# A two-block transformer kernel on one core: x turned once in advance, twelve column tiles beside the first modulation chunks, TensorE's modulation loads moved to the stream queue

## The chip, the cores and the metric

The kernel runs on one core of one Trainium2 chip. The metric is the device time of one execution in microseconds (us). Before the change three runs gave 2236.53, 2239.11 and 2246.66, so the median is 2239.11 us.

## The reference, cut to what matters

The reference runs two blocks on x (256 tokens by 2048 features, float32). The first block has two layers, the second one has one. Only the first block is touched by the change:

```python
for l in range(2):
    mod = silu(c) @ w_ada[l] + b_ada[l]                  # 2048 x 6144 weights
    shift, scale, gate = split(mod, 3)
    h = layernorm(x) * (1 + scale) + shift
    p = h @ w_in[l]                                      # columns: u_f 1024, z_f 1024, cq 512, ckv 256, k_r 64, z_a 1024
    y_f = real(fft2(u_f by groups of 128)) @ w_fmix[l] * silu(z_f)
    q = rmsnorm(cq) @ w_q_b[l];  kv = rmsnorm(ckv) @ w_kv_b[l]
    y_a = attention(q, kv, rope(k_r)) * silu(z_a)        # 8 heads
    x = layernorm(alpha * x + gate * (concat(y_f, y_a) @ w_out[l])) * ln_g[l] + ln_b[l]
```

The modulation is a product of one vector with a matrix: it uses each of its weights once. The other products work on all 256 tokens.

## The kernel before, in words

**Stream.** All large weights but the modulation's lie in one stream of 1 MB chunks (128 partitions by 2048 floats), in the order in which TensorE uses them; layer 0 uses chunks 0 to 56 (`PER_LAYER`, line 57), layer 1 the next 57. SP's queue loads them into a ring of three (`raw`, `RAW`, line 48; `load`, line 328): the load of chunk g waits until chunk g-3 is split. ScalarE casts a chunk to `w_hi` (line 964), VectorE subtracts that to make `w_lo` (line 1378), into one of two slots; a slot is free when TensorE has used the chunk two before (`weights_used`). Each product is three matmuls, lo by hi, hi by lo, hi by hi (`mm3`, lines 409 to 411).

**Modulation.** Layer 0's shift and scale weights are 32 chunks of their own (`ada0`), loaded by SP into a ring of three (lines 320 to 348), with 8 stream chunks between them. TensorE multiplies each chunk in `ada_chunk` (line 586) into one bank. Four chunks make one row of 512 results; ScalarE copies the finished row (`take_row`, line 1006) before TensorE may begin the next, and TensorE turns it into columns (`turn_row`, line 598). VectorE adds the bias (`read_mod0`). The other 64 chunks (layer 0's gate and layer 1's shift and scale, 48 chunks, then layer 1's gate, 16) are loaded by POOL's queue (`weights`, line 369) into a ring of two slots. In layer 0 the even ones go to VectorE (`add_ada`, line 1405; the first of a sum is line 1402), the odd ones to TensorE (`ada_add`, line 539). POOL's loop waits for VectorE's add and loads the next even chunk, then waits for TensorE's add and loads the next odd one, in turn.

**Start of layer 0.** SP loads three modulation chunks, then x. VectorE takes the statistics (line 1496), and stages the normalized x by quarters of 512 features (`stage`, line 1451); TensorE turns a quarter of it after each eighth modulation chunk (`turn_tokens`, line 459). ScalarE applies scale and shift from PSUM (`modulated`, line 989), and VectorE splits the result into `a_hi` and `a_lo` (`split_modulated`, line 1460). From modulation chunk 12 on TensorE does one piece behind each chunk. A piece (`piece`) is one contraction tile of 128 by four column tiles, twelve matmuls of 256 columns. There are eight early column tiles: q's latents (4), kv's latents (2), the rope key, and the first u tile. They take 32 pieces, k outer: 20 beside the modulation chunks, 12 behind.

**Fourier groups.** Then come w_fmix with the channel DFT (chunk 8, four products of 512 columns), the first z tile, and eight groups: a u chunk, the sequence DFT of the group before (`seq_dft`), a z chunk, and the turn to tokens (`to_tokens`). A chunk of this kind is 48 matmuls of 256 columns. ScalarE takes u, the tanh of z, t and y in hi parts, VectorE the lo parts, gates and products, each in an order written out by hand.

**Heads.** For each of eight heads TensorE does `project` (its chunk), the first half of the gate chunk, the turn of the last head's softmax (`turn`, line 746), the second half, the scores, and `attend` of the last head, and in layer 0 then an `ada_add`. VectorE's `head` does the q and k parts, its own `add_ada`, half a split, the turned softmax, the other half, then, when `attend` is done, y (line 1633), the gate (line 1644), v, and the split of the next chunk but one.

**Output projection.** Sixteen chunks of 24 matmuls of 512 columns (`token_chunk`). In layer 0 there are 8 adds of each engine beside them (`W_ADDS`), the sums by rows (`finish_rows`, `turn_rows`, `spread_rows`) and the read of the gate (`read_gate`). VectorE adds the residual by blocks (`z_block`).

## Time and profile before

| what | value |
|---|---|
| median of three runs | 2239.11 us |
| the profiled execution's own time | 2246.86 us |
| its span in the profile | 2245.1 us |
| TensorE busy (matmul) | 2083.1 us, 93% |
| VectorE busy | 1380.8 us, 62% |
| ScalarE busy | 914.7 us, 41% |
| moved by DMA | 462.18 MB, mean 206 GB/s |
| chain that ended last | TensorE 83%, VectorE 9%, DMA 4%, ScalarE 2% |

The span is what the profiler saw of the program on the core; 1.8 us of the execution lie around it. Busy times of different engines overlap, so they do not add up to the span. The chain is followed back from the last instruction, at each step to what released it. Matmuls are pipelined: one of 256 columns shows a duration of 287 ns, though the next starts earlier. The stages of the part that the change touches are: modulation stage of layer 0, 0 to 135.7 us; early tiles and Fourier groups to 305.9; heads to 408.9; output projection to 543.7; layer 1 from there.

### The profile page before, as it was taken

To read this page: it belongs to the slowest core of one execution; us is meant where nothing else is said; L and a number is where in the kernel's file an instruction comes from. 1 tells how busy PE (TensorE), PEld (TensorE's weight loads), DVE (VectorE), ACT (ScalarE), POOL (GpSimd) and SP (SyncE) were. 2 spreads that over 40 slices of the span, in tenths; PEclk is the share of its full clock that TensorE was granted. 3 is DMA by queue.
4 is the path that set the end of the run, shared out by engine and by line. 5 is a ranking of instruction groups with operands and counts; after the bars stand their busy time and mean duration, and the time that the engine had idled before them with its cause. 6 is when DMAs were issued, how large, how long until landed. Compare 5 with 4: busy or idle time off the path is not lost.

```text
span 2245.1 us, 37841 instructions
## 1 busy us (share of the span) xinstructions
PE 2083.1 (93%) x14348; PEld 1885.5 (84%) x14348; DVE 1380.8 (62%) x1895; ACT 914.7 (41%) x1350; POOL 39.0 (2%) x77
## 2 busy tenths in 40 slices
PE   4889899886989999799999899989999999999998
PEld 1578789664989997599998899879989989988986
DVE  4236667557579675779998555555545545555555
ACT  2234345422444564343434333445434434443443
POOL 0000000000000000000000000000000000000000
PEclk7799999988999999889999999999999999999999
DMA  8867767574567544434544455554555555555553
GB/s 360 322 263 300 282 245 290 197 299 187 198 259 284 208 159 169 150 128 173 183 172 150 156 183 185 188 190 147 187 189 186 187 192 188 183 199 191 183 192 131
DMA packets 64198, 462.18 MB, mean 206 GB/s; under 512 B 7120, under 2 KB 7632, under 8 KB 8176
## 3 DMA queue, kind: packets, MB, share of 16 engines
q1 hardware_dynamic: 53696, 385.33, 46.9%
q0 software_dynamic: 10416, 75.63, 8.9%
q8 instruction: 64, 1.05, 0.2%
q14 instruction: 22, 0.18, 0.0%
HBM read 458.83 MB, written 2.10 MB: 205 GB/s over the span
## 4 chain that ended last, share of the span: by engine, by line
PE 83%; DVE 9%; DMA 4%; ACT 2%; issue 2%; DVEq 0%; ACTq 0%; POOLq 0%; SPq 0%; POOL 0%
PE ps L409 26%; PE ps L410 26%; PE ps L411 26%; DMA area<-in_ada 4%; DVE w_lo L1378 3%; PE ps L586 2%; ACT w_hi L964 1%; PE ps L539 1%; PE ps L459 1%; DVE area L1405 1%; DVE X L1758 0%; PE ps L598 0%; DVE X L1752 0%; PE ps L746 0%; DVE ln L1799 0%
## 5 line engine op out<-in xcount | busy, mean ns | idle before, releaser
L1378 DVE TENSOR_TENSOR w_lo<-raw,w_hi 128x1024 fp32r<-128x1024 f32 x658 | 777.5, 1221 | 470.7 <-ACT w_hi L964 469.1
L964 ACT CAST w_hi<-raw 128x1024 fp32r (+1 forms) x658 | 656.8, 1047 | 568.1 <-PE ps L411 567.7
L409 PE MATMUL ps<-a_hi,w_lo 128*128 128x256 f32 (+1 forms) x2912 | 835.9, 287 | 14.3 <-DVE y_lo L1386 5.8
L410 PE MATMUL ps<-a_lo,w_hi 128*128 128x256 f32 (+1 forms) x2912 | 830.8, 285 | 0.0
L411 PE MATMUL ps<-a_hi,w_hi 128*128 128x256 f32 (+1 forms) x2912 | 829.5, 285 | 0.0
L409 PEld LDWEIGHTS ps<-a_hi,w_lo 128*128 128x128 f32 x2912 | 559.7, 192 | 37.6 <-issue 22.2
L411 PEld LDWEIGHTS ps<-a_hi,w_hi 128*128 128x128 f32 x2912 | 559.3, 192 | 0.0
L410 PEld LDWEIGHTS ps<-a_lo,w_hi 128*128 128x128 f32 x2912 | 556.9, 191 | 0.7 <-issue 0.5
L409 PE MATMUL ps<-w_hi,y_lo 128*128 128x512 f32 x768 | 304.7, 397 | 2.6 <-DVE st L1386 2.6
L410 PE MATMUL ps<-w_lo,y_hi 128*128 128x512 f32 x768 | 302.4, 394 | 0.0
L411 PE MATMUL ps<-w_hi,y_hi 128*128 128x512 f32 x768 | 301.8, 393 | 0.0
L409 PEld LDWEIGHTS ps<-w_hi,y_lo 128*128 128x128 f32 x768 | 146.1, 190 | 43.8 <-issue 7.9
L411 PEld LDWEIGHTS ps<-w_hi,y_hi 128*128 128x128 f32 x768 | 146.3, 191 | 31.3
L410 PEld LDWEIGHTS ps<-w_lo,y_hi 128*128 128x128 f32 x768 | 146.3, 191 | 29.7 <-issue 0.2
L1405 DVE SCALAR_TENSOR_TENSOR area<-area,csil 128x2048 f32<-128x2048 f32 x36 | 84.5, 2346 | 29.2 <-DMA area<-in_ada 29.1
L1317 ACT ACTIVATE sc<-ps 128x256 f32<-128x256 f32 x64 | 24.6, 385 | 178.4 <-PE ps L411 178.4
L2015 DVE TENSOR_TENSOR sc<-sc 128x256 f32<-128x256 f32 x64 | 27.3, 426 | 103.0 <-ACT sc L1317 103.0
L409 PE MATMUL ps<-y_hi,w_lo 128*128 128x256 f32 x272 | 78.3, 288 | 9.8 <-DVE y_lo L1931 7.3
L586 PE MATMUL ps<-area,csil 128*1 128x512 f32 x256 | 44.6, 781 | 36.3 <-DMA area<-in_ada 25.1
L410 PE MATMUL ps<-y_lo,w_hi 128*128 128x256 f32 x272 | 77.9, 286 | 0.0
L411 PE MATMUL ps<-y_hi,w_hi 128*128 128x256 f32 x272 | 77.9, 286 | 0.0
L1386 DVE TENSOR_TENSOR st<-ps,st 128x256 fp32r<-128x256 f32 (+1 forms) x98 | 48.0, 505 | 32.4 <-ACT st L1083 22.0
(235 smaller groups left out, 1953.8 us busy)
## 6 DMA issues: line engine op xcount, KB each, us to landing
raw<-in_stream SPq DMA_DIRECT2D x331, 1024.0 KB, 4.8
area<-in_ada POOLq DMA_DIRECT2D x64, 1024.0 KB, 5.4
area<-in_ada SPq DMA_DIRECT2D x32, 1024.0 KB, 7.2
grow<-in_rows POOLq DMA_DIRECT2D x4, 1024.0 KB, 5.0
area<-in_rows POOLq DMA_DIRECT2D x4, 1024.0 KB, 7.0
X<-in_x SPq DMA_DIRECT2D x1, 2048.0 KB, 13.5
out<-X SPq DMA_DIRECT2D x4, 512.0 KB, 2.7
con<-in_consts SPq DMA_DIRECT2D x1, 129.5 KB, 13.1
```

What stands on the lines that cost most here:

```text
L409: pe.matmul(o, w[1], a[0], start=first, stop=False, skip_group_check=shared)
L410: pe.matmul(o, w[0], a[1], start=False, stop=False, skip_group_check=shared)
L411: return pe.matmul(o, w[0], a[0], start=False, stop=last, skip_group_check=shared)
L459: o = pe.transpose(bank(turn_banks(n, q)[i // 2], i % 2 * T + t * P, P), src, ident)
L539: o = pe.matmul(ps[32 * j:32 * j + 1, ROW_BANK[r] * 512:(ROW_BANK[r] + 1) * 512], csil[:, KT + n % KT:KT + n % KT + 1], ada_ring[:, CH + j ...
L586: o = pe.matmul(ps[32 * k:32 * k + 1, 2 * 512:3 * 512], csil[:, at:at + 1], ada0_slot(c % 3)[:, k * 512:(k + 1) * 512], start=s == 0, stop ...
L964: ac.copy(to, raw[:, bass.ds((g % RAW) * CH + h * n, n)]).then_inc(hi_ready, 1)
L1317: ac.activation(sc[:, b * T:(b + 1) * T], bank(b), ACT.Relu).then_inc(f_relu, 1)
L1378: ve.tensor_tensor(to, raw[:, bass.ds((g % RAW) * CH + h * n, n)], hi.bitcast(F32), ALU.subtract).then_inc(lo_ready, 1)
L1386: return ve.tensor_tensor(out_, exact, hi.bitcast(F32), ALU.subtract)
L1405: ve.scalar_tensor_tensor(out=ada_acc, in0=chunk, scalar=c, in1=ada_acc, op0=ALU.mult, op1=ALU.add).then_inc(ada_step, 1)
L2015: ve.tensor_tensor(s, r, r, ALU.mult).then_inc(f_sq, 1)
```

## The change

In words, part by part:

- **Order of the first loads.** SP loads x and the constants before the first three modulation chunks.
- **x turned in advance.** VectorE stages all four quarters at once; TensorE turns them after modulation chunks 2 to 5; ScalarE copies the turned quarter to a hi part (in `y_hi`, not yet used), VectorE subtracts to make the lo part (in `y_lo`). `modulated` then reads the hi part, and VectorE adds the lo part times scale, one operation for each tile.
- **Twelve early column tiles.** u tiles 1 and 2, z tiles 0 and 1, kv's latents, the rope key, u tile 0, and q's latents, three chunks to a quarter. That makes 48 pieces. Behind modulation chunk c, pieces up to (c - 10) * 3 // 2 are done, so 31 by chunk 31. SP loads 9 stream chunks in this stage. The last quarter is mixed with the w_fmix products (`last_quarter`). u tiles 1 and 2 are kept in hi and lo, z tile 1's gate is kept in `grow`. Layer 1 gets the same tiles and order.
- **Groups.** Group loops are written out in full on all engines; groups begin with z tile 2, then u tile 3.
- **TensorE's modulation chunks.** POOL's loop loads only the even chunks for layer 0's time. SP loads the odd ones (`row_weights`) between stream chunks, into the same slot of the ring. TensorE's adds stand behind the chunks in `PE_ADDS` (6 in the groups, 10 in the heads, 8 in the output projection), in the heads ahead of `attend`.
- **VectorE's adds.** In layer 0: 5 in the groups, 7 in the heads, 12 in the output projection (before: 9, 7 and 8). In layer 1: two in each of groups 4 to 7 and one in each head (before: two in each of the eight groups).
- **Banks and order of the row sums** follow from that.

The diff, cut to its core:

```diff
-FIRST = 8
-L_FMIX = FIRST
-L_DFT = FIRST + 2
-L_FOUR = FIRST + 1
+FIRST = 3
+L_FMIX = 4 * FIRST - 1
+L_Z2 = L_FMIX + 2
+L_DFT = L_Z2 + 1
+L_FOUR = L_DFT + 1 - 6
 L_HEAD = L_FOUR + 2 * GROUPS
...
-W_ADDS = ((1, 3, 4, 6, 8, 10, 12), (3, 4, 5, 6, 7, 8, 10, 12))
+PE_ADDS = tuple(L_FOUR + i for i in (7, 8, 10, 11, 12, 14)) \
+    + tuple(L_HEAD + i for i in (1, 3, 5, 7, 8, 9, 11, 12, 13, 15)) \
+    + tuple(L_OUT + i for i in (2, 4, 5, 7, 8, 10, 11, 12))
...
             sp.dma_start(vec[:, :], vectors).then_inc(vec_in, 16)
+            sp.dma_start(X[:, :].rearrange("p (t d) -> p t d", t=2), x.rearrange("(t p) d -> p t d", p=P))\
+                .then_inc(x_in, 16)
+            sp.dma_start(con[:, :], consts).then_inc(con_in, 16)
             for c in range(3):
                 sp.dma_start(ada0_slot(c), ada0[c]).then_inc(ada0_landed[c], 16)
...
+            early = {9: 0, 11: 1, 14: 2, 17: 3, 19: 4, 22: 5, 25: 6, 27: 7, 30: 8}
             for c in range(3, ADA0):
+                if c in early:
+                    g = early[c]
+                    load(g, g % 2, g >= 2)
                 sp.wait_ge(ada0_used, c - 2)
                 sp.dma_start(ada0_slot(c % 3), ada0[c]).then_inc(ada0_landed[c % 3], 16)
...
+            def row_weights(i):
+
+                sp.dma_start(ada_ring[:, CH:2 * CH], ada[2 * i + 1]).then_inc(ada_rowed, 16)
+
+            for g in range(9, PER_LAYER + 1):
+                load(g, g % 2, True)
+                if g == L_FMIX + 1:
+                    sp.wait_ge(ada0_used, ADA0)
+                    row_weights(0)
+                if g - 5 in PE_ADDS[:-1]:
+                    i = PE_ADDS.index(g - 5) + 1
+                    sp.wait_ge(ada_pe, i)
+                    row_weights(i)
...
             weights(0, 0)
-            weights(1, 1)
-            pool.wait_ge(ln_lo, 8)
+            pool.wait_ge(y_mul, 2)
             row(grow[:, :], R_GATE, grow_in)
             with pool.Fori(1, 3 * KT // 2) as i:
-                for par in range(2):
-                    pool.wait_ge((ada_step, ada_pe)[par], i)
-                    weights(2 * i + par, par)
+                pool.wait_ge(ada_step, i)
+                weights(2 * i, 0)
...
+                if 2 <= c < 6:
+                    turn_tokens(0, c - 2)
...
-                if c % 8 == 7:
-                    turn_tokens(0, c // 8)
-                if c >= 12:
-                    n = c - 12
-                    if n == 0:
-                        pe.wait_ge(ln_var, NORM["meta"] + 1)
-                    piece(0, n // 8, n % 8 // 4, n % 4)
...
+                if c == 10:
+                    pe.wait_ge(ln_var, NORM["meta"] + 1)
+                    pe.wait_ge(xn_l, 4)
+                while p < (c - 10) * 3 // 2:
+                    piece(0, p // 12, p % 12 // 4, p % 4)
+                    p += 1
+            while p < 36:
+                piece(0, p // 12, p % 12 // 4, p % 4)
+                p += 1
+                if p == 34:
+                    turn_row(ADA0 // 4 - 1)
+            last_quarter(0)
...
+            def last_quarter(l):
+
+                pieces(l, 3, 0)
+                pieces(l, 3, 1, range(2))
+                if l:
+                    pe.wait_ge(fm_y, 2 * KT)
+                else:
+                    pe.wait_ge(col_in, 4)
+                half(l * PER_LAYER + L_FMIX, 1)
+                fourier_weights(l, (0, 1))
+                pieces(l, 3, 1, range(2, 4))
+                fourier_weights(l, (2, 3))
+                pieces(l, 3, 2)
...
+                def later(o):
+
+                    if l == 0 and o in PE_ADDS:
+                        ada_add(2 * PE_ADDS.index(o) + 1)
+
+                def group_u(q):
+                    g = L_FOUR + 2 * q
+                    chunk(G + g, slot_of(g), bank(0), a_ops)
+                    later(g)
...
+                to_tokens(0)
+                group_z(2)
+                seq_dft(0)
+                to_tokens(1)
...
+                for q in range(4, GROUPS):
+                    group_u(q)
+                    seq_dft(q - 1)
+                    group_z(q)
                     to_tokens(q)
...
                     project(h, first)
+                    if l == 0:
+                        later(L_HEAD + 2 * h)
...
-                    if l == 0 and h == HEADS - 1:
-                        finish_rows(3)
+                    if l == 0:
+                        later(L_HEAD + 2 * h + 1)
+                        if h == 3:
+                            finish_rows(2)
                     if not first:
                         attend(h - 1, second)
...
+                    later(L_OUT + c)
+                    if l == 0 and c == 4:
+                        finish_rows(3)
+                    if l == 0 and c == 6:
+                        turn_rows(4, 10)
...
+            for q in range(3):
+                split(3 * q, q % 2, q % 2)
                 ac.wait_ge(col_in, q + 1)
                 modulated(0, q)
+                take_row(2 * q + 2)
+                split(3 * q + 1, (q + 1) % 2, (q + 1) % 2)
+                split(3 * q + 2, q % 2, q % 2)
+                take_row(2 * q + 3)
...
+                if n == 0:
+                    for m in (2 * i, 2 * i + 1):
+                        one = pair[:, m % 2 * T:(m % 2 + 1) * T]
+                        o = ve.scalar_tensor_tensor(out=one, in0=y_lo[:, m * T:(m + 1) * T].bitcast(F32),
+                                                    scalar=mod[:, KT + m:KT + m + 1], in1=one, op0=ALU.mult, op1=ALU.add)
+                    own.link(o)
...
+                    if l:
+                        add_ada(7 * KT // 2 + h, h % 2, 2 * KT + h)
+                    elif h < 3:
+                        add_ada(10 + 2 * h, 0, 5 + h)
+                    elif h > 3:
+                        add_ada(8 + 2 * h, 0, 4 + h, 3 if h == 4 else 0)
...
-                    if l == 0 and c in W_ADDS[0]:
-                        n = 2 * KT + 2 + 2 * W_ADDS[0].index(c)
-                        add_ada(n, 0, n // 2)
+                    if l == 0 and (c < 4 or 5 <= c < 13):
+                        n = 24 + 2 * c - 2 * (c > 4)
+                        add_ada(n, 0, n // 2, 4 if c == 5 else 0)
```

## Rows read from the trace of the kernel before

**Rows 1.** The page: its span, and TensorE's and the others' busy time.
```profile
span 2245.1 us, 37841 instructions
PE 2083.1 (93%) x14348; PEld 1885.5 (84%) x14348; DVE 1380.8 (62%) x1895; ACT 914.7 (41%) x1350; POOL 39.0 (2%) x77
```
**Rows 2.** Stages: window, length, busy PE, PEld, DVE, ACT, POOL; clock, DMA share, GB/s.
```profile
0.00:52.91 52.91, 22.65 (x123) 5.44 (x124) 22.83 (x54) 12.75 (x19) 0.20 (x4) 0.72 0.88 355
52.91:71.40 18.49, 15.87 (x96) 10.04 (x96) 1.45 (x2) 2.48 (x3) 0.00 (x0) 0.78 1.01 424
71.40:88.40 17.00, 14.38 (x88) 9.17 (x88) 4.74 (x9) 4.41 (x7) 0.00 (x0) 0.80 0.67 256
...
124.51:135.68 11.17, 11.17 (x77) 7.23 (x78) 0.91 (x1) 0.00 (x0) 0.00 (x0) 0.85 0.84 344
...
305.86:408.86 103.00, 101.69 (x850) 93.65 (x849) 78.22 (x120) 57.53 (x119) 6.89 (x13) 1.00 0.79 295
408.86:543.73 134.87, 119.01 (x538) 87.47 (x538) 77.80 (x80) 39.18 (x49) 8.47 (x16) 0.91 0.66 250
```
**Rows 3.** Timeline of TensorE in the modulation stage: start, length, instruction, idle before.
```profile
52.91 1.88 PE L586 MATMUL ps<-area,csil 128*1 128x512 f32 x8 [2.42 <-DMA area<-in_ada]
...
71.40 1.88 PE L586 MATMUL ps<-area,csil 128*1 128x512 f32 x8 [2.62 <-ACT rs L1006]
73.21 1.87 PE L598 MATMUL ps<-csil,rs 128*128 128x1 f32 x8
...
80.59 1.04 PE L586 MATMUL ps<-area,csil 128*1 128x512 f32 x8
```
**Rows 4.** Timeline of VectorE, 0 to 56 us: statistics of x, rotary table.
```profile
16.23 4.84 DVE L1496 BATCH_NORM_STATS2 ln<-X 128x6 f32<-128x512 f32 x8 [12.24 <-DMA X<-in_x]
...
39.06 0.35 DVE L1535 TENSOR_SCALAR rope<-rope,con 128x256 f32<-128x256 f32 x1 [3.93 <-ACT rope L1016]
```
**Rows 5.** Timeline of TensorE in one head: add, gate chunk, turn, scores, add.
```profile
348.92 1.04 PE L539 MATMUL ps<-area,csil 128*1 128x512 f32 x8
...
354.88 0.33 PE L409 MATMUL ps<-a_hi,w_lo 128*128 128x256 f32 x1
...
357.79 0.60 PE L746 MATMUL ps<-con,sc 128*128 128x128 f32 x4
...
361.03 0.28 PE L409 MATMUL ps<-st 128*128 128x256 f32 x1
...
363.27 1.04 PE L539 MATMUL ps<-area,csil 128*1 128x512 f32 x8
```
**Rows 6.** Timeline of VectorE in the same head: add, y, split.
```profile
357.98 2.35 DVE L1405 SCALAR_TENSOR_TENSOR area<-area,csil 128x2048 f32<-128x2048 f32 x1
...
363.47 0.42 DVE L1633 SCALAR_TENSOR_TENSOR sc<-ps,zs 128x256 f32<-128x256 f32 x1 [0.27 <-PE ps L411]
...
365.01 2.36 DVE L1378 TENSOR_TENSOR w_lo<-raw,w_hi 128x1024 fp32r<-128x1024 f32 x2 [0.33 <-ACT w_hi L964]
```
**Rows 7.** Landings: two POOL loads (180 us), one SP load (141), POOL in output projection.
```profile
DMA to landing us min/median/max: 5.1/6.1/7.0
...
DMA to landing us min/median/max: 4.9/4.9/4.9
...
DMA to landing us min/median/max: 5.0/6.8/9.2
```
**Rows 8.** Timeline of TensorE: two modulation adds behind a wait.
```profile
272.34 1.89 PE L539 MATMUL ps<-area,csil 128*1 128x512 f32 x8 [9.01 <-DMA area<-in_ada]
...
471.44 1.88 PE L539 MATMUL ps<-area,csil 128*1 128x512 f32 x8 [3.78 <-DMA area<-in_ada]
```
**Rows 9.** The view of rows 2, the 4 us behind the second of these waits.
```profile
472.00:476.00 4.00, 4.00 (x15) 2.17 (x8) 2.39 (x2) 0.00 (x0) 0.53 (x1) 0.50 0.87 279
```
**Rows 10.** Timeline of VectorE: its first modulation add in the output projection.
```profile
424.71 1.28 DVE L1402 TENSOR_SCALAR area<-area,csil 128x2048 f32<-128x2048 f32 x1
```
**Rows 11.** TensorE's waits in layer 1, 568.64 to 760 us: total, times, longest.
```profile
PE ps L409 <- DVE st L1386: 4.8, 3, 2.2
```

More of the change, by code:

```diff
@@ L1726, in head @@
                     ve.reciprocal(stat[:, 6:8], stat[:, 4:6]).then_inc(s_sum, 1)
-                head(0, True, l == 0)
-                with own.loop(1, HEADS - 1, 1) as h:
-                    head(h, False, l == 0)
-                head(HEADS - 1, False, False)
+                for h in range(HEADS):
+                    head(h, h == 0)
                 def z_block(j, t):
```

571 lines of the change are left out of this document (318 added, 253 removed).

## The prediction, made before the changed kernel was seen

> **What bounds the kernel now.** I read the page first [rows 1]: TensorE is busy 93% of the span, so nearly everything that takes work off its path, or stops it, moves the end. Then the engines' time by stage [rows 2]. In the first 135.7 us 32 chunks of layer 0's shift and scale weights stream in, and TensorE is paced by others. In the heads of layer 0 (305.86 to 408.86) it is busy 101.69 of 103.00, in the output projection behind them (408.86 to 543.73) only 119.01 of 134.87. What to see in [rows 3]: in the first stage each row of four modulation chunks costs TensorE a wait of 2.62 for ScalarE's copy of the row, and then some microseconds at half clock (a chunk's matmuls take 1.88 instead of 1.04).
>
> **Part 1: x turned in advance, twelve tiles.**
> (a) SP's queue now loads x before the modulation chunks. VectorE got x at 16.23 [rows 4], behind 3 MB of chunks; a megabyte more of queue lands 2.5 later (below, [rows 7]), so x comes 7.5 earlier, at 8.7. From x to the finished rotary table took 39.06 - 16.23 = 22.8; four stagings and four subtractions are put in between, 4 x (1.0 + 1.2) as estimates from the 0.42 and 0.6 us operations of [rows 6] and [rows 4] by their sizes. The table is ready near 41, the first modulated pair near 47.6. Chunk 12, at 52.91 before [rows 3], starts near 50: **-2.9**.
> (b) From chunk 12 on, rows of four chunks carry six pieces instead of four. A 256-column matmul costs TensorE (361.03 - 354.88 - 0.45 for the turn at 357.79) / 48 = 0.1187 [rows 5], a piece of twelve 1.42. A row at full clock: four chunks 4.0, the turned row 1.0 (1.87 at half clock, [rows 3]), six pieces 8.6, together 13.6. ScalarE now copies the row before its cast and not behind it, and TensorE has a piece to do meanwhile, so the waits of 2.62 go. Five rows took 135.7 - 52.9 = 82.8 (a plain one 17.00, [rows 2]); they would take 68 at full clock and 85 at this row's mean clock of 0.80. I take 75, since the long waits came just before the half clock: **-7.8**. In this stage SP loads 9 stream chunks instead of 8.
> (c) 31 pieces are done by the last modulation chunk instead of 20. The products in all are the same, so afterwards 11 x 12 x 0.1187 = **-15.7**. The last quarter keeps its waits (for the last modulation and for the Fourier weights, now behind a Tanh table load) and gets one more, on the split of its third chunk: **+1.0**. VectorE's two corrections for each of eight pairs (0.42 each) lie in its idle time; without that cover they cost 7.
> Part 1 together: -25.4. Bounds: -32 (full clock) to -15 (clock of before).
>
> **Part 2: the odd modulation chunks on the stream queue.** That queue is in order. Let a be the stream chunk after which TensorE did the add before. The next odd chunk is issued behind stream load a+5, which waits until chunk a+2 is split, and that split begins only when a is consumed. A lone 1 MB load by SP lands in 4.9; of two issued 0.6 apart, the second landed 7.0 + 0.6 - 5.1 = 2.5 after the first [rows 7]. So the odd chunk lands 7.3 to 7.4 after the split of a+2. Two chunks later that is in time; at the very next chunk it is not. Neighbours in the new list, by offset in the layer: 16-17, 19-20, 20-21 (groups), 32-33, 33-34, 36-37, 37-38 (heads), 45-46, 48-49, 51-52, 52-53 (output projection).
> Heads. Project runs from 348.92 + 1.0 to 354.88, 5.0; the gate chunk to 361.03; scores 1.42, attend 0.71, add 1.0 [rows 5]. The add now stands ahead of attend. VectorE's chain y, gate, v, split begins when attend ends (363.2) and ends at 365.01 + 2.36, 4.1 later [rows 6]. For 32-33: scores 1.4, add 1.0, row sum 1.0, attend 0.7 and 4.1 make 8.2; the load goes at 8.4 and lands at 15.7. TensorE is there after 4.1 + 5.0 = 9.1 and waits 6.6; for 36-37, one row sum less on both sides, the same. For 33-34 the split of 35 is cut in two by the softmax turn, which now stands behind the stalled add: 7.6 + half a chunk 2.85 + turn 0.45 + copy and subtraction 1.4 + half a split 1.2 = 13.5, landed 21.0. TensorE is there at 7.6 + 2.85 + 0.45 + 2.85 + 1.42 = 15.2 and waits 5.8; 37-38 the same. Together 24.8. Nothing is gained in exchange, the loads were in time here. After a wait of 3.78 an add took 1.88 [rows 8], and the clock stood at 0.50 for the next 4 us [rows 9]; I count 2.6 lost after each wait, 10 for four. Heads: **+35**. From below, with the split 4.1 after the chunk and no clock lost, 9; from above 45.
> Groups. Gone is the wait of 9.01 [rows 8] with some 3 of half clock. New, by the same sum with the add not ahead of attend: 3.8 at 16-17, 5.5 at 19-20, and 5 of clock: **+2** (-8 to +8).
> Output projection. VectorE makes 12 adds here instead of 8, all through one ring slot, each 2.35 [rows 6]; the next load is issued 0.6 behind it. TensorE, with 5.7 for a chunk and 1.0 for an add, is slower than this cycle only if a load lands within 3.7. POOL's loads here took 5.0 at least and 6.8 in the median [rows 7], many issued two at once; alone I take 5.8, a cycle of 8.7. The first add ends 18.2 into the stage (424.71 + 2.35, [rows 10]); eleven more take 95; the two last chunks and a row sum 12: 125. The neighbours' waits lie partly beside this; I count 10 of them: 135, against 134.87. **0** (-15 to +26).
>
> **Part 3: layer 1.** Its 16 adds stood two to a group; eight now go to the heads, where layer 0 bore one each. TensorE waited 4.8 there on VectorE's subtractions [rows 11], and lost some clock: **-4** (0 to -8).
>
> Sum: -25.4 + 2 + 35 + 0 - 4 = +8 on the profiled execution's 2246.9 (span 2245.1). That execution lies 7.8 above the median of the runs, so the same 8 goes on 2239.1: **2247**.
>
> **Rivals.** A measurement of this kernel can tell about 0.5%, 11 us, from no change.
> A, the forecast: what the first stage gains is given back in the heads. 2247, its own range 2229 to 2262. Chance 0.38.
> B, slower: the output projection becomes VectorE's chain of modulation loads. Place: its adds from chunk 1 to chunk 12. If SP's two loads for each chunk delay POOL's, a landing takes 8.2, between the median and the longest 9.2 [rows 7], and not 5.8; 11 x 2.4 = 26 makes 2273. It decides from a landing of 6.1 on. For it speaks that median, against it that many of these loads went in pairs. 0.32. The Trainium skill (DMA: Bandwidth & Descriptors, Queues, rings and completion order) says that each DMA engine goes round the queues that have work, packet by packet. By that rule POOL's load would share its way with SP's two, and B would hold.
> C, faster: the odd chunks land in time in the heads. Then the heads cost -1 and the total is 2211. For it: SP's new wait blocks nothing; against it: the sum above. 0.22.
> D, the change does not do what it says: the first stage's loads bind, and the products are not free. At 355 GB/s (0 to 52.91, [rows 2]) its 45.5 MB last 128 and start 3 late; chunk 31 ends 7 later than I take, the total is 2254. Against it: 424 GB/s from 52.91 to 71.40 [rows 2]. 0.08. The skill's rule (same page, Where 436 GB/s comes from) that reads from HBM bind a core at about 358 GB/s is this case. The 424 of this trace disagrees with it.
>
> **How the numbers follow.** A: same 0.34, faster and slower 0.02 each; B: slower 0.30, same 0.02; C: faster 0.20, same 0.02; D: slower 0.06, same 0.02. Faster 0.22, same 0.40, slower 0.38. The range reaches down to C and up to near B: 2211 to 2270.
>
> **What would show it.** TensorE waits 6 us before its modulation matmuls at four places in the heads, ended by SP's load, and the heads take near 138 instead of 103; in the first stage no wait of 2.62, rows near 15, the last chunk done near 125; in the output projection VectorE waits for its load at nearly every add. If TensorE waits nowhere in layer 0's heads, A falls and C holds; if the output projection takes over 145, B; if the first stage ends later than 132, D.

## The result, and the profile after

The changed kernel took 2256.68 us in the median of six runs (2253.37 to 2257.75), the kernel before 2239.21 in the median of six (2236.53 to 2246.66). The ratio is 1.0072, 95% interval 1.0056 to 1.0088: slower by 0.78%, 17.5 us. The forecast was 2247, the range 2211 to 2270. The profiled execution of the changed kernel took 2257.66, 1.0 above its median, that of before 7.7 above its own, so the two spans differ by 10.8 only; the last experiment deals with the other 6.7.

The page of the changed kernel, its span and busy times; it answers to [rows 1].

```profile
span 2255.9 us, 37129 instructions
PE 2078.6 (92%) x14348; PEld 1879.9 (83%) x14348; DVE 1391.3 (62%) x1913; ACT 921.5 (41%) x1355; POOL 26.2 (1%) x53
```

TensorE's busy time fell by 4.5 us (2083.1 before) and its idle time rose by 15.3 (from 162.0 to 177.3). The granted clock averages 0.956 over the span, before it was 0.955: the half clock that left the first stage came back in later ones.

The stages of the changed kernel, with the columns of [rows 2]: to modulation chunk 12, the 20 chunks behind it, early tiles and groups to the first head's add, heads, output projection.

```profile
0.00:51.22 51.22, 28.76 (x159) 10.39 (x159) 29.42 (x64) 16.86 (x23) 0.20 (x4) 0.81 0.97 390
51.22:120.70 69.48, 69.34 (x550) 48.88 (x549) 25.82 (x36) 20.26 (x26) 0.00 (x0) 0.99 0.97 399
120.70:274.11 153.41, 134.77 (x1066) 124.63 (x1062) 93.26 (x126) 64.16 (x101) 4.36 (x8) 0.94 0.61 228
274.11:412.39 138.28, 113.39 (x874) 99.15 (x873) 76.19 (x117) 57.85 (x119) 3.17 (x6) 0.89 0.60 227
412.39:558.51 146.12, 121.89 (x546) 88.46 (x546) 86.90 (x83) 39.07 (x49) 6.87 (x13) 0.88 0.73 273
```

The same five stages of the kernel before, in its profiled execution. Two of the rows stand in [rows 2]; here are the other two that the accounting needs:

```profile
52.91:135.68 82.77, 72.29 (x445) 46.26 (x446) 15.12 (x22) 13.76 (x20) 0.00 (x0) 0.78 0.81 324
135.68:305.86 170.18, 154.97 (x1236) 141.69 (x1235) 105.55 (x131) 68.68 (x107) 11.79 (x22) 0.96 0.70 260
```

So the change gained 31.8 us up to the first head's add (305.86 to 274.11), paid 35.3 in the heads (103.00 to 138.28) and 11.3 in the output projection (134.87 to 146.12), and gained 4.0 behind it (1701.4 to 1697.4, each span less the end of the projection): +10.8 in all.

The modulation stage, TensorE's timeline of the changed kernel; it answers to [rows 3].

```profile
65.81 1.04 PE L655 MATMUL ps<-area,csil 128*1 128x512 f32 x8
66.78 1.05 PE L667 MATMUL ps<-csil,rs 128*128 128x1 f32 x8
```

No wait of 2.62 stands before the first chunk of a row, and chunk and turn take 1.04 and 1.05, not 1.88 and 1.87: the clock is whole (0.99 in the window above, 0.78 before).

TensorE's waits of the changed kernel in the heads, then in the output projection (what waited, for what: total, times, longest):

```profile
PE ps L608 <- DMA area<-in_ada: 23.6, 4, 6.3
...
PE ps L608 <- DMA area<-in_ada: 15.2, 4, 7.7
PE ps L452 <- DVEq L1555: 5.4, 1, 5.4
PE ps L617 <- DVE area L1536: 3.5, 1, 3.5
```

Two of those adds in TensorE's timeline, one of the groups and one of the heads; they answer to [rows 8]:

```profile
226.03 1.89 PE L608 MATMUL ps<-area,csil 128*1 128x512 f32 x8 [10.03 <-DMA area<-in_ada]
```
```profile
330.46 1.88 PE L608 MATMUL ps<-area,csil 128*1 128x512 f32 x8 [6.33 <-DMA area<-in_ada]
```

Each took 1.88 or 1.89, not 1.04: it ran at half clock, as after the waits of before. L608 is TensorE's modulation add, L452 a matmul on stream weights, L617 the row sum, L1536 VectorE's modulation add, L1555 its read of the gate. In the heads only a wait of 1.3 us stands beside these, as before (103.00 less 101.69 busy). So 23.6 of the 35.3 that the heads lost are waits, and 11.7 are busy time (113.39 against 101.69). Part of that is half clock, and part is more work: TensorE's adds in the heads, before and then in the changed kernel (eight records are one add; behind the count stand busy us, the mean ns of one, and the idle time before):

```profile
L539 PE MATMUL ps<-area,csil 128*1 128x512 f32 x56 | 7.3, 591 | 0.0
L608 PE MATMUL ps<-area,csil 128*1 128x512 f32 x80 | 13.8, 769 | 23.6 <-DMA area<-in_ada 23.6
```

These are 7 adds and 10, so three more, some 2.9 us at full clock; they came out of the groups, which had 9 and have 6. That leaves some 8.8 for the half clock. SP's seven loads for adds in the heads, the four that were waited for among them:

```profile
DMA to landing us min/median/max: 6.8/6.8/6.9
```

Each of the four was issued 0.4 us behind a stream load (the two at 323.1 and 323.5, for instance, landed 4.6 and 6.9 after their issue).

### The profile page after: what moved, and what is told of

It is laid out like the page before. It is cut to its first block, busy times and chain, and to the rows that moved or that the text cites. A ratio compares the mean times of both kernels' runs of the same rounds, so it can differ in the third digit from the quotient of the medians.

```text
span 2255.9 us, 37129 instructions
## 1 busy us (share of the span) xinstructions
PE 2078.6 (92%) x14348; PEld 1879.9 (83%) x14348; DVE 1391.3 (62%) x1913; ACT 921.5 (41%) x1355; POOL 26.2 (1%) x53
## 4 chain that ended last, share of the span: by engine, by line
PE 77%; DVE 12%; DMA 7%; ACT 2%; issue 1%; SPq 0%; ACTq 0%; DVEq 0%; POOLq 0%
PE ps L452 25%; PE ps L453 24%; PE ps L454 24%; DMA area<-in_ada 6%; DVE w_lo L1509 4%; DVE area L1536 2%; PE ps L655 1%; PE ps L608 1%; ACT w_hi L1038 1%; DVE st L1517 1%; DVE X L1940 0%; PE ps L502 0%; DMA raw<-in_stream 0%; DVE X L1934 0%; ACT sc L1269 0%
## 5 line engine op out<-in xcount | busy, mean ns | idle before, releaser
L452 PE MATMUL ps<-a_hi,w_lo 128*128 128x256 f32 (+1 forms) x2912 | 830.4, 285 | 10.6 <-DVE w_lo L1509 6.7
L452 PEld LDWEIGHTS ps<-a_hi,w_lo 128*128 128x128 f32 x2912 | 555.1, 191 | 32.2 <-issue 21.9
L452 PE MATMUL ps<-w_hi,y_lo 128*128 128x512 f32 x768 | 306.0, 398 | 8.0 <-DVEq L1555 5.4
L452 PEld LDWEIGHTS ps<-w_hi,y_lo 128*128 128x128 f32 x768 | 146.9, 191 | 49.4 <-issue 9.7
L1536 DVE SCALAR_TENSOR_TENSOR area<-area,csil 128x2048 f32<-128x2048 f32 x36 | 84.5, 2346 | 32.2 <-DMA area<-in_ada 32.2
L452 PE MATMUL ps<-y_hi,w_lo 128*128 128x256 f32 x272 | 78.7, 289 | 8.8 <-DVE y_lo L2111 5.8
L608 PE MATMUL ps<-area,csil 128*1 128x512 f32 x192 | 31.7, 739 | 53.5 <-DMA area<-in_ada 53.4
```

What stands on the lines that cost most here:

```text
L452: pe.matmul(o, w[1], a[0], start=first, stop=False, skip_group_check=shared)
L608: o = pe.matmul(ps[32 * j:32 * j + 1, ROW_BANK[r] * 512:(ROW_BANK[r] + 1) * 512], csil[:, KT + n % KT:KT + n % KT + 1], ada_ring[:, CH + j ...
L1536: ve.scalar_tensor_tensor(out=ada_acc, in0=chunk, scalar=c, in1=ada_acc, op0=ALU.mult, op1=ALU.add).then_inc(ada_step, 1)
```

## The experiments

Times of one run each are compared with the changed kernel's profiled 2257.7; where there is a median, it is of four runs. The six runs of the changed kernel spread over 4.4 us, so a single run that differs by 6 or 7 says little by itself; there the stage that was aimed at carries the argument.

**1. The row load one stream load earlier.**

```diff
-                if g - 5 in PE_ADDS[:-1]:
-                    i = PE_ADDS.index(g - 5) + 1
+                if g - 4 in PE_ADDS[:-1]:
+                    i = PE_ADDS.index(g - 4) + 1
```

> TensorE's modulation weights are asked for one stream load earlier, ahead of the stream load they follow now. In the changed kernel the loads for two adds in neighbouring places are issued 0.4 us behind a stream load and land 6.8 to 6.9 us later, and TensorE waits 6.33, 5.56, 6.19 and 5.50 us for them in heads and 10.03 us at chunks 19 to 20 of the groups, with the granted clock at half after each. Theory: the place of the issue is all that is wrong. Issued at the end of the add before, alone, the load lands in 4.9 us while TensorE does its next chunk (some 6.4 us): the four waits (23.6 us) and the half clock behind them (some 10 us) go, and heads take 103 to 106 us instead of 138.3; of the groups' 14.7 us of waits more than half goes; in all 2200 to 2220 us, below the kernel before. Rival 1: the adds themselves, ahead of the attend step and of the scores, are what costs: heads stay above 125 us and the time moves by less than 10 us. Rival 2: SyncE now waits for an add and holds the stream loads behind it, so TensorE waits for its stream chunks instead: the idle places move, heads 120 us or more and the time 2235 or more.

Measured: 2208.25 us in the median (2204.88 to 2208.83), beside 2238.65 for the kernel before; ratio 0.9853, 0.9826 to 0.9880. The stages from the first kernel's same marks, groups, heads and output projection:

```profile
120.50:261.14 140.64, 132.02 (x1066) 123.64 (x1063) 93.06 (x126) 63.85 (x101) 4.35 (x8) 0.99 0.67 250
261.14:371.87 110.73, 106.34 (x874) 95.70 (x873) 76.15 (x118) 57.74 (x119) 3.17 (x6) 0.98 0.75 282
371.87:507.96 136.09, 117.55 (x546) 85.81 (x546) 86.63 (x83) 39.18 (x49) 6.85 (x13) 0.92 0.79 295
```

TensorE's waits in its heads, and the landing of SP's loads there:

```profile
PE ps L608 <- DMA area<-in_ada: 3.1, 1, 3.1
...
DMA to landing us min/median/max: 4.7/6.4/7.8
```

Two characters of the source are worth 48 us. The theory holds in its main point, and both rivals fall: with the same adds in the same places, asking earlier for their loads turned four waits of 23.6 us in the heads into one of 3.1, and no wait for a stream chunk came in exchange. The stream loads did get slower: those of the heads landed in 6.0 us in the median instead of 4.8. Of the gain, 27.6 lies in the heads (138.3 to 110.7), 12.8 in the groups, 10.0 in the output projection. One detail of the theory was off: the loads do not land in 4.9, but in 6.4 in the median. They are in time because they start sooner, not because they are much faster (6.8 in the changed kernel). Heads stayed 7.7 above before and not 0 to 3: 3.1 is the one wait, some 1.7 the half clock behind it (3.4 us long), and some 2.9 the three more adds that stand there (874 records against 850, eight to an add).

**2. The add behind attend.**

```diff
+                    if not first:
+                        attend(h - 1, second)
                     if l == 0:
                         later(L_HEAD + 2 * h + 1)
                         if h == 3:
                             finish_rows(2)
-                    if not first:
-                        attend(h - 1, second)
```

> In heads, TensorE's second modulation add (and the finishing of one row) stands behind the attend step of the head before instead of ahead of it; loads as in the changed kernel. If the four head waits are set by the landing of the load (asked for 0.4 us behind a stream load, 6.8 us to land), the add comes some 1 us later in its head and the load for the next one too: the waits stay between 4 and 6 us each, heads take 132 to 140 us (138.3 now), the time falls by 8 us at most. If it is the place ahead of attend that costs, since VectorE and ScalarE idle while TensorE waits there, heads fall to 125 us or less and the time by over 12 us.

Measured: 2249.96, 7.7 less, with heads of 135.0 (273.95 to 408.93). TensorE's waits in its heads:

```profile
PE ps L608 <- DMA area<-in_ada: 19.4, 4, 5.4
```

4.5 to 5.4 each. The place ahead of attend cost a microsecond a time (23.6 less 19.4, by four), and the rest of each wait is the lateness of the load. The theory's numbers for the waits, the stage and the time are all met, the time as far as one run tells.

**3. Short loads for VectorE in the output projection.**

```diff
-            with pool.Fori(1, 3 * KT // 2) as i:
+            with pool.Fori(1, 13) as i:
                 pool.wait_ge(ada_step, i)
                 weights(2 * i, 0)
+            with pool.Fori(13, 3 * KT // 2) as i:
+                pool.wait_ge(ada_step, i)
+                pool.dma_start(ada_ring[:, 0:CH // 4],
+                               ada[bass.ds(2 * i, 1), :, 0:CH // 4].rearrange("a p n -> (a p) n")).then_inc(ada_landed[0], 16)
```

> GpSimd's loads of modulation weights from the fourteenth on (those that VectorE adds in the output projection, and one before) move a quarter of each chunk only; the rest of the buffer keeps older weights, so the sums of these chunks are not computed in full. VectorE's adds are as long as before, and everything else is the changed kernel's. Theory (the chain of load and add on VectorE made the output projection 146.1 us instead of 134.9): the landings fall from 6.3 us on average to some 3 us, VectorE's waits for them (26 us there) go nearly all, TensorE's waits of 3.47 to 7.71 us at 452 to 519 us shrink under 2 us each, and the output projection takes 128 to 136 us: the time falls by 10 to 18 us. Rival: the adds and the gate read themselves (2.3 us each, queued ahead of a split) hold TensorE up: the output projection stays above 142 us.

The kernel leaves out three quarters of the weights of those chunks, so it is a probe and not a version. Measured: 2250.99, 6.7 less and not 10 to 18; the heads, which the edit does not aim at, were 2.0 longer in this execution. Its output projection:

```profile
415.28:550.73 135.45, 116.59 (x546) 84.66 (x546) 86.53 (x83) 39.08 (x49) 6.97 (x13) 0.94 0.62 229
```

VectorE's waits for these loads in the output projection, in the changed kernel, then here; and GpSimd's landings, the same two:

```profile
DVE area L1536 <- DMA area<-in_ada: 26.6, 8, 6.1
```
```profile
DVE area L1540 <- DMA area<-in_ada: 10.7, 5, 4.7
```
```profile
DMA to landing us min/median/max: 5.0/5.4/9.3
```
```profile
DMA to landing us min/median/max: 3.2/4.1/5.3
```

The stage fell by 10.7, to within a microsecond of before, inside the theory's 128 to 136 and far from the rival's 142: VectorE's adds took as long as before, so it is the loads in the chain load, add, load on VectorE that made it long. The landings came down to 4.1 only, not to 3; VectorE still waited 10.7 us of 26.6; and TensorE's waits for its own row loads stayed at 4.2 to 5.0 (three), not under 2. With the time these are four numbers of the theory that were too good. The first experiment reached 136.1 by the other end, with full loads on VectorE and TensorE's loads early. The stage is long where both chains are late at once; mending either one brings it to about 136.

**4. Five early pieces for four chunks instead of six.**

```diff
-                while p < (c - 10) * 3 // 2:
+                while p < (c - 10) * 5 // 4:
```

> In the modulation stage five pieces of the first mixer's chunks are laid beside every four modulation chunks from the tenth on, instead of six: 26 pieces by the last chunk instead of 31, so that five (each 12 products, 1.42 us at full clock) run behind it. If TensorE's work alone sets the stage, nothing is lost: the last modulation chunk ends some 7 us earlier (120.7 now, 114 then) and the first head's add stands at 274 us as now. If the weight loads (1 MB each) set it, the last chunk ends at 118 or later and the five pieces are added behind: the first head's add at 277 to 281 us, the time 3 to 7 us longer.

Measured: 2279.04, 21.4 more, and the first head's add at 292.65: far outside both. TensorE's waits in the stage, and ScalarE's timeline at the same time:

```profile
86.32 1.04 PE L655 MATMUL ps<-area,csil 128*1 128x512 f32 x8 [1.85 <-DMA area<-in_ada]
97.14 1.28 PE L655 MATMUL ps<-area,csil 128*1 128x512 f32 x8 [2.62 <-ACT rs L1085]
116.64 1.03 PE L655 MATMUL ps<-area,csil 128*1 128x512 f32 x4 [3.73 <-ACT rs L1085]
```
```profile
94.61 1.99 ACT L1038 CAST w_hi<-raw 128x1024 fp32r<-128x1024 f32 x2 [10.62 <-PE ps L454]
96.50 0.58 ACT L1085 COPY rs<-ps 128x512 f32<-128x512 f32 x1
```

ScalarE stood 10.62 us before a cast that may only begin when pieces have freed the slot, and the copy of the finished row (L1085), for which TensorE waited, was queued behind it. Around the ends of the three waits the granted clock was at half for 3.4, 6.8 and 10.2 us, the last time from 1.8 us before the wait ended.

**5. The same, with the row copy ahead of that cast.**

```diff
                 split(3 * q + 1, (q + 1) % 2, (q + 1) % 2)
-                split(3 * q + 2, q % 2, q % 2)
                 take_row(2 * q + 3)
+                split(3 * q + 2, q % 2, q % 2)
```

> As the kernel with five early pieces for four modulation chunks (2279 us), but ScalarE copies each odd row ahead of its cast of the third chunk of a quarter instead of behind it. There TensorE waited 2.62 us at 94.5 and 3.73 us at 112.9 for that copy, while ScalarE stood at the cast, which waits until pieces have freed its slot; after these the clock stood at half for 6.8 and 10.2 us. Theory: the loss of 22 us came from this order on ScalarE's queue and the half clock behind it, not from the fewer pieces: both waits go, the last modulation chunk starts by 119 instead of 130, the first head's add stands at 274 to 281 us instead of 292.7, and the time is 2256 to 2265. Rival: with fewer pieces TensorE outruns the weight loads (it waited 1.85 us at 84.5 for one), the clock falls for that alone: the time stays above 2270.

Measured: 2270.45, first head's add at 286.64. From chunk 12 to the last, then to the first head's add:

```profile
52.07:125.30 73.23, 66.32 (x489) 44.39 (x488) 22.83 (x33) 18.61 (x25) 0.00 (x0) 0.93 0.89 361
125.30:286.64 161.34, 142.08 (x1126) 131.94 (x1122) 96.81 (x130) 66.18 (x103) 4.37 (x8) 0.95 0.59 223
```

The first wait for the copy is gone; one of 3.01 stayed at 106.85, in the fifth row, with 10.2 us of half clock from just before its end. The theory's marks were missed (the time, and the first head's add at 281 or earlier), and the rival's (a time above 2270) was met by 0.45 us; but the half clock came with the wait for the copy, not with the short waits for loads that the rival names. ScalarE's timeline shows why the wait stayed:

```profile
103.65 2.00 ACT L1038 CAST w_hi<-raw 128x1024 fp32r<-128x1024 f32 x2 [8.07 <-PE ps L454]
107.27 2.07 ACT L1068 ACTIVATE grow<-y_hi,mod 128x256 f32<-128x256 f32 x4 [1.62 <-DVE mod L1698]
109.25 0.56 ACT L1085 COPY rs<-ps 128x512 f32<-128x512 f32 x1
```

It is the other copy, `take_row(2 * q + 2)`, which the edit did not move: it too is queued behind a cast that stands for TensorE's pieces. The 3.73 of the fourth experiment was a wait for that copy as well. So 6.0 of the 18.5 us lay in the part of ScalarE's order that was changed here. Of the 12.5 left, 7.9 is the second window, near the five pieces done later (5 x 1.42 = 7.1), and some 4 the first one, which did not get shorter by the pieces it lost. With six pieces a row takes 13.9 us and TensorE hardly stops (69.34 busy of 69.48); with five it waits 0.7 to 1.2 for loads (at 68.3, 76.1, 85.6 and 103.6 us in this kernel), and what it left undone is paid behind. That TensorE would win nothing by doing less with both copies out of the way is not shown: by an estimate from these rows the wait of 3.0 and some 4.8 for the half clock behind it (9.7 us at half) would come off the 73.2, which leaves about 65.4, 4.1 less than with six pieces, against the 7.9 behind.

**6. Row sums a chunk later, on top of the first.**

```diff
-    + tuple(L_OUT + i for i in (2, 4, 5, 7, 8, 10, 11, 12))
+    + tuple(L_OUT + i for i in (2, 4, 5, 7, 8, 10, 11, 13))
...
-                    if l == 0 and c == 4:
+                    if l == 0 and c == 5:
                         finish_rows(3)
...
-                    if l == 0 and c == 13:
+                    if l == 0 and c == 14:
                         finish_rows(4)
```

> On top of the first experiment (row loads one stream load earlier, 2208 us): in the output projection the two row sums that wait for VectorE's adds stand one chunk later (behind chunks 5 and 14 instead of 4 and 13), with the turn, the copy and the read that follow from them, and TensorE's last modulation add stands behind chunk 13 instead of 12. In that experiment TensorE waited 3.10 and 6.66 us there for VectorE's add and 2.24 us for its last load, each with 3 to 7 us at half clock behind it. Theory (the remaining cost in the output projection is where TensorE meets VectorE's chain, not the chain's length): these three waits go to under 1 us, the output projection takes 121 to 128 us instead of 136.1, in all 2193 to 2202 us. Rival (the chain of load and add on VectorE is as long as the stage, so the wait only moves): the next thing that needs VectorE, the split of a stream chunk or the last row sum, waits as long, the output projection stays above 132 us and the time above 2204.

Measured: 2206.36 (2205.07 to 2207.51), ratio 0.9850, 0.9834 to 0.9867. TensorE's waits in its output projection:

```profile
PE ps L452 <- DVEq L1555: 7.0, 1, 7.0
PE ps L452 <- DVE w_lo L1509: 4.5, 2, 3.5
PE ps L608 <- DMA area<-in_ada: 3.0, 2, 1.6
```

The waits for the row sums are gone (9.8 in the first experiment), but the stage takes 132.45, just above the rival's 132, and the time is above its 2204: the gate read is waited for 7.0 instead of 5.2, and a split 3.5. Most of the wait moved. VectorE is late, whatever asks for it next. The stage is 3.6 shorter than in the first experiment, but the runs of the two overlap, so no gain in time is claimed.

**7. One of VectorE's adds moved out of the output projection, on top of that.**

```diff
+                    elif q == GROUPS - 1:
+                        add_ada(10, 0, 5)
...
-                    elif h < 3:
-                        add_ada(10 + 2 * h, 0, 5 + h)
+                    elif h < 2:
+                        add_ada(12 + 2 * h, 0, 6 + h)
...
-                    if l == 0 and (c < 4 or 5 <= c < 13):
+                    if l == 0 and c in (0, 2, 3, *range(5, 13)):
```

> On top of the one before: one of VectorE's adds is moved from the output projection (behind its chunk 1, ahead of the gate read) to the last Fourier group, the adds between move up by one place, and the first row sum stands in head 2 instead of head 3. TensorE waited 5.25 us at the fifth chunk of the output projection for the gate read, which stood on VectorE behind an add that waited 5.89 us for its load. Theory: the wait for the gate read goes, with some 1.7 us of half clock, and nothing comes in its place, since VectorE is idle 13% of the last group: 4 to 7 us less than the one before. Rival: the added one in the last group waits for its load (5 us at least behind the add before it) ahead of a split that TensorE needs, and a wait of 3 us or more appears at the first head: no gain.

The diff is cut; the row sum that moves from head 3 to head 2, and the numbers of the adds between, are left out.

Measured: 2203.25 (2200.68 to 2210.47), ratio 0.9845, 0.9822 to 0.9869. Heads and output projection:

```profile
263.88:378.01 114.13, 107.94 (x873) 96.07 (x872) 76.18 (x117) 57.83 (x119) 3.17 (x6) 0.97 0.72 273
378.01:502.33 124.32, 114.12 (x546) 84.22 (x546) 85.08 (x83) 39.19 (x49) 6.33 (x12) 0.96 0.82 315
```

The wait for the gate read went, and the projection is 8.1 shorter, 10.6 below that of the kernel before as first profiled. TensorE still waits 7.8 us in it for splits. The heads took back 3.7 (waits for row loads of 4.9 us instead of 2.8, with half clock at each), which the theory had excluded; the rival's wait at the first head did not come. The runs of this version and the one before overlap, so of the 3 us between their medians nothing is claimed, and the theory's 4 to 7 are not shown.

**8. The last version again, and its fifth group add a chunk later.**

```diff
-PE_ADDS = tuple(L_FOUR + i for i in (7, 8, 10, 11, 12, 14)) \
+PE_ADDS = tuple(L_FOUR + i for i in (7, 8, 10, 11, 13, 14)) \
```

> The last version once more, on the same chip as its two variants, so that they can be compared: 2200 to 2206 us, the stages within 3 us of before (first head's add 261 to 265, heads 111 to 115, output projection 123 to 126).

> On top of the last version (2203 us): TensorE's fifth modulation add stands behind the z chunk of the sixth group instead of the u chunk before it. There its load was issued 0.4 us behind a stream load, after VectorE's late split, landed 7.9 us later and TensorE waited 4.33 us, with clock to lose behind it. Theory: with one chunk more between the adds the load is in time, the wait goes and none of over 1 us takes its place in the groups: first head's add at 258 to 260 us instead of 263.9, the time 3 to 6 us less. Rival: the next pair (now neighbours one chunk later) waits in its place, 3 us or more: same time.

Measured: 2204.87 (2201.64 to 2209.66) for the version again, 2196.64 (2194.11 to 2204.13) with the add moved, ratio 0.9797, 0.9765 to 0.9829: the fastest complete version, 1.7 to 2.4% below the kernel before. (One of its four runs lies among those of the version again.) Its profiled execution is the slowest of its four, so the profile can't say well where the 8 us are. It shows a wait of 2.90 at the new place, where the version again has 4.80 at the old one: part of the theory, part of the rival. The version again also shows a wait of 3.71 at 252.86, for a subtraction that stands on VectorE in the last groups, which its first profile did not have. The next experiment's kernel, with the same order there, shows one of 3.55 at the same place; the first experiment and the row sums' version, without the added add, show none, nor does the kernel with the fifth add moved. The added add is a likely cause, then, but not of every execution, and it is not tested. It put the first head's add at 267.4, outside what was expected (the other marks were inside, the heads at 115.3 by a hair outside).

**9. Short loads on that version.** The edit is that of the third experiment.

> The last version (2203 us), with GpSimd's loads from the fourteenth on moving a quarter of each chunk only, so that those chunks are not summed in full. In its output projection (124.3 us) TensorE still waited 2.94, 1.07, 3.64 and 1.20 us, the larger two for splits that stand on VectorE behind an add that waited 2.9 to 6.1 us for its load. Theory (VectorE's chain of loads is the last thing that binds there): VectorE's waits for loads go, TensorE's waits fall to under 3 us in sum, the output projection takes 114 to 119 us (16 chunks of 6 to 6.5 us, eight adds of 1.0, the row sums): 6 to 10 us less. Rival: the waits come from VectorE's own work (adds of 2.35, blocks of 2.1, splits of 1.2): 122 us or more stay.

Again a probe that leaves part of the sums out. Measured: 2197.10, 6.2 to 7.8 below the two medians of that version, and the stage inside the theory's 114 to 119. Its output projection and TensorE's waits in it:

```profile
384.84:499.30 114.46, 112.90 (x546) 84.79 (x546) 85.97 (x84) 39.20 (x49) 6.45 (x12) 0.96 0.73 270
```
```profile
PE ps L456 <- DVE st L1521: 1.3, 1, 1.3
PE ps L456 <- DVE w_lo L1513: 1.2, 1, 1.2
```

TensorE is busy 112.90 of 114.46. VectorE's work alone (86 us, as much as in the changed kernel) holds nothing up. Its waits for loads did not all go, as the theory had it (14.0 us in six, from 27.0 in nine), but what was left of them hardly stopped TensorE. The loads of its one ring slot are what is left in that stage, 10 to 11 us. Short loads also leave more room to SP's loads (TensorE's 2.0 us of waits for its row loads went too), and the two effects are not told apart.

**10. The kernel before once more.** No edit.

> The kernel before, once more. Its profiled execution took 2246.9 us, 7.7 above the median of its runs, while that of the changed kernel lay 1.0 above its own. If that was chance, this execution is within 4 us of 2239 and one stage alone shows where the 7 us were: by the windows the first 135.7 us, where clock and loads differ from run to run, rather than the stages at full clock. If the profile itself costs this kernel 7 us, it is at 2246 again, in the same stages.

Measured: 2235.40. Its five stages:

```profile
0.00:53.74 53.74, 27.23 (x123) 7.15 (x124) 22.81 (x54) 12.76 (x19) 0.20 (x4) 1.00 0.87 348
53.74:130.52 76.78, 65.53 (x445) 42.49 (x446) 15.11 (x22) 13.76 (x20) 0.00 (x0) 0.87 0.88 351
130.52:296.99 166.47, 155.28 (x1235) 142.20 (x1236) 105.15 (x131) 68.69 (x107) 11.75 (x22) 0.97 0.70 266
296.99:399.99 103.00, 101.70 (x850) 93.65 (x849) 78.53 (x120) 57.43 (x119) 6.88 (x13) 1.00 0.78 295
399.99:531.72 131.73, 117.99 (x538) 86.88 (x538) 77.66 (x79) 39.19 (x49) 8.45 (x16) 0.91 0.67 256
```

So the profile does not cost this kernel 7 us: this one was profiled too and is below all six of the result, and the first one's excess was chance. But it was not in one stage: 6.0 us lay in the rows of modulation chunks, 3.7 in the groups, 3.1 in the output projection (1.4 elsewhere went the other way, 11.4 in all), and nothing in the heads, where TensorE hardly stops. As far as two executions tell, it varies where TensorE is paced by loads (the start, to chunk 12, was 0.8 longer here).

## Why the forecast was right and where it was not

The case forecast, A, is what the runs show: the first stage's gain is given back in the heads. B's mechanism came on top of it, at about half of B's price. Against both executions of the kernel before (the one profiled, and the one of the last experiment, nearer to the median), in us:

| step | forecast | against the profiled | against the second |
|---|---|---|---|
| (a) chunk 12 starts | -2.9 | -1.7 | -2.5 |
| (b) twenty chunks, 75 forecast | -7.8 | -13.3 | -7.3 |
| (c) and groups: -15.7 + 1.0 + 2 | -12.7 | -16.8 | -13.1 |
| heads | +35 | +35.3 | +35.3 |
| output projection | 0 | +11.3 | +14.4 |
| layer 1 and the rest | -4 | -4.0 | -4.6 |
| sum | +8 | +10.8 | +22.2 |

**(a), (b).** Chunk 12 started at 51.22, not 50. VectorE had x at 9.15 (8.7 forecast) and the first modulated pair was ready at 46.5 (47.6 forecast), so the path that (a) follows was on time, even early. What held TensorE was another: chunk 11 waited 3.16 us for its own load and began at 46.54, and the clock was at half from 32.0 to 52.5. The rows took 69.5 us, near the 68 worked out for full clock and not the 75 that I chose between that and the clock of before. I had kept some half clock as a habit of the stage; it was gone together with the waits. With (c) kept at its forecast, part 1 was not -25.4 but about -30 on the profiled execution (-1.7 - 13.3 - 15.7 + 1.0). On the second execution the difference is close to the forecast, but only because that one had lost less clock itself.

**(c) and groups.** TensorE waited 4.66 at 16-17 (forecast 3.8) and 10.03 at 19-20 (5.5): VectorE does the latents' operations (205.6 to 211.7) and an add of its own ahead of the split there, which the sum left out, and the stream load, with the row load 0.4 behind it, went late: the row load was issued at 217.1, when TensorE had already stood for 1.1 us, and landed some 9 us later. So the waits were 5.4 more than forecast, and yet the line comes out 4.1 better on the first execution and 0.4 on the second. Some 2.9 of that is the three adds that moved from here to the heads, which neither term counts; the rest is not divided between (c) and the groups. That this line fits is partly luck.

**Heads.** Forecast waits of 6.6, 5.8, 6.6 and 5.8, measured 6.33, 5.56, 6.19 and 5.50; landings at 6.8 to 6.9 behind a stream load. The way it was reckoned, by following one chunk's split to the load's issue and landing, was right to 0.4 us a wait. That the stage's sum fits to 0.3 is in part luck: the waits (23.6 for 24.8) and the half clock (8.8 for 10) were each a little less than reckoned, and three more adds, 2.9 us, were not in the sum at all. Rival C's condition, odd chunks in time, is what the first experiment made true: 2208, against its 2211. Its price fits by cancelling too: the heads cost 7.7 there and not -1, and the groups gained 29.5 (140.64 against 170.18) where the forecast has 12.7.

**Output projection: the term that failed.** The prediction has "alone I take 5.8, a cycle of 8.7" and "I count 10 of them: 135, against 134.87", so a term of 0. The first add ended 18.2 into the stage, as forecast (428.24 + 2.34 - 412.39). The eleven further adds took 110.5, 10.0 each, not 8.7 (the last began at 538.75 and took 2.35). The landings were 6.3 on average (of the eleven), 0.5 more than taken, and in some cycles VectorE was not free when the load was there: it waited 26.6 us for eight of the eleven. The rest behind the last add took 17.4, not 12. The parts 18.2, 110.5 and 17.4 fill the 146.1 by themselves, so the 10 counted for the neighbours' waits lay beside the chain. Put as terms of the sum: the cycle cost 15 more than taken (some 5 of it the landings, some 10 VectorE's delays), the tail 5, and 10 too many stood for the neighbours. B's condition (a landing of 6.1 or more; the prediction does not show where that figure comes from) was met by the mean of 6.3 but not by the median of 5.4, its sign (a stage over 145) came at 146.1, but its price assumed landings of 8.2. That it is the loads and not VectorE's own work, the third and ninth experiments show. The Trainium skill's rule that was weighed for B (DMA: Bandwidth & Descriptors, Queues, rings and completion order: engines go round the queues that have work) agrees with the direction here: the three longest landings (9.3, 8.8 and 7.6) are of loads issued 1.4 to 4.0 us behind a load of SP that had yet to land, the three of 5.0 of loads issued when SP's last had landed or was within 1.1 us of it; no run here shows the packets' order itself.

**D.** It did not hold: the stage ended at 120.7, not past 132, at 399 GB/s. The Trainium skill's 358 GB/s (DMA: Bandwidth & Descriptors, Where 436 GB/s comes from) is again not what these rows show.

**The median.** I put the +8 on the median since the profiled execution lay 7.8 above it (7.7 with all six runs). That is sound only if a kernel's lead comes evenly. The excess of that execution lay in stages that the change rebuilds, so it went away with them, and the difference of the medians was 17.5. The distance from 2247 to 2256.7 is thus some 7 from this step and some 3 net from the stages: the output projection's 11.3, most of it cancelled by (b) and (c), which came 9.6 better than forecast on that execution. The last column shows it without the excess: the stages then miss by 14, and the output projection is all of it.

## What to carry to other kernels

When loads of one engine are put into another's in-order queue, write down for each the event that releases the issue, and count from there: here the place behind stream load a+5 instead of a+4 turned a gain of 30 us into a loss of 17. When work moves between stages, count it in both: three adds of TensorE's were missing from two of the sums here. A wait that goes in a row sum or a gate read may only show who is late; look for the engine that all of them wait for, and give its loads room before moving the meeting places. And take out the excess of a profiled execution by stage, not by the whole.

## What the runs showed of the hardware

- TensorE's granted clock fell to half at every wait of 3 us and more in layer 0 of the changed kernel behind chunk 12 (ten, of 3.47 to 10.03 us). At the four in the heads it stood at half for 6.8 to 10.2 us, from 1.2 to 4.9 us before the wait ended, so that 3.1 to 5.7 us of it fell on work. In the first experiment it fell a microsecond behind the end of the wait of 3.08, for 3.4 us. Shorter waits did it at times: one of 1.85 in the fourth experiment and most of those of 2.62 in the kernel before. The twenty modulation chunks, with no wait of 2.62 left, ran at 0.99 where they had 0.78 with waits of 2.62.
- A 1 MB load that SP issued 0.4 us behind another one landed in 6.8 to 6.9 us in the heads (the load ahead of the one at 323.5 took 4.6) and in 8.9 to 9.0 at 197.6 and 217.1 us in the groups.
- A load of a quarter of the size (256 KB) by GpSimd's queue landed in 4.1 us in the median, the 1 MB one in 5.4: three quarters less in bytes brought only a quarter less in time, beside SP's traffic.
- Weights streamed at 399 GB/s over 69 us, with TensorE busy 69.34 of 69.48: the stage is balanced between the two, so neither fewer pieces nor faster loads alone would shorten it much. For the loads that is a reading, not a test; for the pieces the fourth and fifth experiments are the test, with ScalarE's second row copy still in the way.
